# Mixer stage of a two-block kernel: six banks for the first products, values in pairs of blocks, the convolution in two pieces, and an engine order rewritten around them

## The reference, cut to what matters

```python
# second block, one layer; xl 512 latent tokens, xc 256 context tokens
pl = modulate(rmsnorm(xl), sh1, sc1) @ w_in;  pc = modulate(rmsnorm(xc), ...) @ w_in
# mLSTM, 4 heads of 128: q, k from a 3x3 depthwise convolution and silu; v, output gate, input/forget gates
qk = silu(dwconv2d(p[..., :2*W], conv_w, rows, cols))
h_ml = rmsnorm_head(forward scan + backward scan of (q, k, v, gates)) * sigmoid(o)
# HGRN, 4 heads of 128: q = silu(.), decays for two directions, v, gate g
h_hg = rmsnorm_head(forward scan + backward scan of (q, k, v, log decays)) * silu(g)
xl = xl + g1 * (concat(h_ml, h_hg) @ w_out)
# then a convolutional feed-forward part and the final norm
```

## Time and profile before

| | |
|---|---|
| time, median of 3 runs (lowest to highest) | 1871.69 us (1871.32 to 1872.26) |
| the profiled execution: its time, its span | 1873.64 us, 1871.9 us |
| PE busy | 1733.9 us, 93% of the span |
| DVE, ACT, POOL busy | 1176.7, 730.2, 461.1 us |
| mean granted TensorE clock | 0.965 of full speed |
| the stage of the change | about 953 to 1462 us of the span |

### The profile page before, as it was taken

One profiled execution on the slowest core, in us unless ns is written; L12 is line 12 of the kernel. 1 busy time (PEld: TensorE's weight loads), 2 busy tenths in 40 slices (PEclk: granted clock), 3 DMA queues, 4 the chain that ended last, 5 costly groups with the idle time before them and its releaser, 6 DMA issues.

```text
span 1871.9 us, 21559 instructions
## 1 busy us (share of the span) xinstructions
PE 1733.9 (93%) x7645; PEld 1321.3 (71%) x7645; DVE 1176.7 (63%) x2193; ACT 730.2 (39%) x1176; POOL 461.1 (25%) x448
## 2 busy tenths in 40 slices
PE   7998898999989999999998988988898899999996
PEld 3446654588867888888757766877756488888885
DVE  5968653344447755775655377576774587777776
ACT  3154556433443311331253272735361433333224
POOL 2732200030020100110000122221320066656552
PEclk9998799999999999999999999998999999999999
DMA  5264200143333554454303211111311323322311
GB/s 148 68 126 113 76 4 1 45 130 88 108 102 136 184 174 135 161 186 147 123 13 91 57 45 34 53 38 34 102 46 34 101 90 113 113 91 85 118 46 45
DMA packets 185537, 168.69 MB, mean 90 GB/s; under 512 B 17639, under 2 KB 168867, under 8 KB 185051
## 3 DMA queue, kind: packets, MB, share of 16 engines
q1 hardware_dynamic: 173083, 128.19, 22.4%
q0 software_dynamic: 11808, 39.29, 7.1%
q10 hardware_dynamic: 560, 0.12, 0.0%
HBM read 155.83 MB, written 6.31 MB: 87 GB/s over the span
## 4 chain that ended last, share of the span: by engine, by line
PE 71%; DVE 14%; ACT 8%; issue 4%; DMA 1%; POOL 1%; POOLq 0%; DVEq 0%; SPq 0%; ACTq 0%
PE bank L1509 27%; PE bank L1928 18%; PE bank L1620 3%; DVE arena L2678 2%; PE bank L1302 2%; PE bank L1814 2%; DVE arena L3340 2%; PE bank L1669 2%; PE bank L1462 2%; PE bank L1448 2%; PE bank L1625 1%; PE bank L1404 1%; PE bank L1806 1%; DVE arena L3428 1%; PE bank L1660 1%
## 5 line engine op out<-in xcount | busy, mean ns | idle before, releaser
L3582 DVE SCALAR_TENSOR_TENSOR arena<-bank,ffn_taps,arena 128x441 f32<-128x441 f32 (+2 forms) x352 | 220.2, 686 | 79.3 <-ACT arena L2638 79.3
L3049 DVE TENSOR_TENSOR w_lo<-ring,w_hi 128x2048 fp32r<-128x2048 f32 x52 | 119.2, 2292 | 117.0 <-ACT w_hi L2213 113.2
L1509 PE MATMUL bank<-h_lo,w_hi 128*128 128x512 f32 x448 | 176.6, 394 | 3.2 <-DVE w_lo L3049 1.8
L2213 ACT CAST w_hi<-ring 128x2048 fp32r<-128x2048 f32 x52 | 99.2, 1907 | 176.4 <-PE bank L1509 176.4
L1509 PE MATMUL bank<-hT_hi,w_hi 128*128 128x512 f32 x384 | 153.5, 400 | 6.5 <-DVE h_lo L3135 5.8
L1160 POOL TENSOR_TENSOR w_lo<-ring,w_hi 128x2048 fp32r<-128x2048 f32 x21 | 99.7, 4745 | 168.9 <-ACT w_hi L2611 168.9
L1509 PE MATMUL bank<-act_hi,w_hi 128*128 128x512 f32 x352 | 137.9, 392 | 0.2
L1509 PE MATMUL bank<-act_lo,w_hi 128*128 128x512 f32 x352 | 131.8, 389 | 0.0
L1928 PE MATMUL bank<-hT_hi,w_hi 128*128 128x512 f32 x336 | 130.8, 389 | 0.3 <-POOL w_lo L1160 0.3
L1928 PE MATMUL bank<-h_lo,w_hi 128*128 128x512 f32 x336 | 130.7, 389 | 0.0
L1928 PE MATMUL bank<-hT_hi,w_lo 128*128 128x512 f32 x336 | 130.7, 389 | 0.0
(11 more groups left out here) (577 smaller groups left out, 4037.5 us busy)
## 6 DMA issues: line engine op xcount, KB each, us to landing
ring<-in_w_up SPq DMA_DIRECT2D x76, 512.0 KB, 4.6
arena<-in_w_mod POOLq DMA_DIRECT2D x48, 512.0 KB, 4.2
ring<-in_w_in SPq DMA_DIRECT2D x72, 256.0 KB, 3.2
ring<-in_w_down SPq DMA_DIRECT2D x32, 512.0 KB, 4.2
ring<-in_w_in SPq DMA_DIRECT2D x30, 512.0 KB, 3.9
arena<-in_w_down SPq DMA_DIRECT2D x22, 512.0 KB, 4.4
ring<-in_w_out SPq DMA_DIRECT2D x8, 512.0 KB, 3.8
ring<-in_w_out SPq DMA_DIRECT2D x16, 256.0 KB, 3.1
```

The lines of the kernel that those rows point to most:

```text
L1509: ins = pe.matmul(out, u[:, n % SLOTS, cols], v[:, k, :], start=start and k == w[0][0] and m == 0, stop=stop and k == w[-1][0] and m == 2)
L2213: sc.copy(w_hi[:, n % SLOTS, :], ring[:, n % SLOTS, :]).then_inc(hi_ready, 1)
L3049: ve.tensor_tensor(w_lo[:, n % SLOTS, :], ring[:, n % SLOTS, :], value(w_hi[:, n % SLOTS, :]), ALU.subtract)\
L3582: return ve.scalar_tensor_tensor(o[:, ys, xs], x[:, yt, xt], ffn_taps[:, at:at + 1], o[:, ys, xs], ALU.mult, ALU.add)
```

## The change

It has five parts, all in the order of work and the places of tiles; no arithmetic is added or taken away.

1. **Banks.** A new kind "first" goes round six banks (3, 4, 0, 1, 2, 7) and holds all tiles of the prelude up to mlk of head 0, but zc. The decays of head 1 and the rounds use "dense" as before. In the rounds y2 goes to bank 7 (with the HGRN output "o"), y3 to the kind "ml".
2. **Values in pairs.** The four latent blocks of v go in two pairs, each with all high products first; in the last pair low products follow each k. The signals that free chunk slots (`chunk_used` at k = 2, 4, 6) are now given at the first block of the last pair.
3. **Convolution in two pieces.** The query's nine taps (piece 0) run at n = 9, ahead of the first `ml_divide`; the keys' twelve instructions (piece 1) at n = 0 of the round that uses them, after the second `ml_divide`.
4. **Roundings ahead.** In the prelude ACT rounds zf, zb and Vb0 to Vb2 earlier, and DVE takes the lows of zf and zb between the scans of the gate rows, after a memset of `sums` that moves ahead of them. In the rounds ACT rounds g between two halves of `ml_weights`, and mlq ahead of the silus.
5. **Bank reads ahead.** The flips (n = 7) come before the scores s4 and s5 on PE. DVE does `ml_probs` before `assemble` at n = 7 and 8, and `heads_out` ahead of mo's low part at n = 8 (at n = 7 in the last round, ahead of the reads of A6 and A7). ACT copies mlc before mlk.

```diff
--- before.py
+++ after.py
@@ -133 +133,2 @@
-        places = {"unit": (0, 1, 2), "dense": (3, 4), "ml": (5, 6), "o": (7,), "out": (0, 1, 2, 5)}[kind]
+        places = {"unit": (0, 1, 2), "first": (3, 4, 0, 1, 2, 7), "dense": (3, 4), "ml": (5, 6), "o": (7,),
+                  "out": (0, 1, 2, 5)}[kind]
@@ -136,0 +138,5 @@
+    def decays(kind, i):
+        tile(kind, "zf", i)
+        tile("ml", "zc", i)
+        tile(kind, "zb", i)
+
@@ -138 +144 @@
-        tile("dense", "v", 0, b)
+        tile("first", "v", 0, b)
@@ -140 +146 @@
-        tile("dense", "gr", m)
+        tile("first", "gr", m)
@@ -142,8 +148,3 @@
-        tile("dense", "v", 0, b)
-    def decays(i):
-        tile("dense", "zf", i)
-        tile("ml", "zc", i)
-        tile("dense", "zb", i)
-
-    decays(0)
-    tile("dense", "q", 0)
+        tile("first", "v", 0, b)
+    decays("first", 0)
+    tile("first", "q", 0)
@@ -151,2 +152,2 @@
-        tile("dense", "v", 1, b)
-    tile("dense", "cols")
+        tile("first", "v", 1, b)
+    tile("first", "cols")
@@ -154,2 +155,2 @@
-        tile("dense", name, 0)
-    decays(1)
+        tile("first", name, 0)
+    decays("dense", 1)
@@ -178,0 +180,3 @@
+            if n == 7 and i:
+                tile("dense", "fh", i - 1)
+                tile("dense", "fm", i - 1)
@@ -185,3 +188,0 @@
-            if n == 7 and i:
-                tile("dense", "fh", i - 1)
-                tile("dense", "fm", i - 1)
@@ -194 +195 @@
-                    tile("ml", "y", i, b)
+                    tile(("o", "ml")[b - 2], "y", i, b)
@@ -1670 +1671 @@
-                            if (m, b, k, v) == (1, 0, 0, 0) or (last and v == 0 and k in (2, 4, 6)):
+                            if (m, b, k, v) == (1, 0, 0, 0) or (last and n + v == 0 and k in (2, 4, 6)):
@@ -1843,2 +1844,2 @@
-            for b in range(CT, ST):
-                mixer_values(0, [b])
+            for b in range(CT, ST, 2):
+                mixer_values(0, [b, b + 1])
@@ -1851,2 +1852,2 @@
-            for b in range(CT, ST):
-                mixer_values(1, [b])
+            for b in range(CT, ST, 2):
+                mixer_values(1, [b, b + 1])
@@ -1891,0 +1893,3 @@
+                    if n == 7 and i:
+                        hg_flip(i - 1)
+                        ml_flip(i - 1)
@@ -1898,3 +1901,0 @@
-                    if n == 7 and i:
-                        hg_flip(i - 1)
-                        ml_flip(i - 1)
@@ -2488 +2489 @@
-            def ml_weights(i):
+            def ml_weights(i, half):
@@ -2490 +2491 @@
-                for n in range(2 * ST):
+                for n in range(half * ST, (half + 1) * ST):
@@ -2510,2 +2511 @@
-            for b in range(CT + 1, ST - 1):
-                value_copy(0, b)
+            value_copy(0, CT + 1)
@@ -2513 +2512,0 @@
-            value_copy(0, ST - 1)
@@ -2514,0 +2514,2 @@
+            for b in range(CT + 2, ST):
+                value_copy(0, b)
@@ -2515,0 +2517 @@
+            mix_high("Vb0")
@@ -2517,0 +2520,2 @@
+            mix_high("Vb1")
+            mix_high("Vb2")
@@ -2519,2 +2523 @@
-            for k in range(4):
-                mix_high(f"Vb{k}")
+            mix_high("Vb3")
@@ -2528 +2530,0 @@
-            value_copy(1, 4)
@@ -2530 +2531,0 @@
-            value_copy(1, 5)
@@ -2531,0 +2533,2 @@
+            value_copy(1, 4)
+            value_copy(1, 5)
@@ -2540 +2542,0 @@
-            ml_copy("mlk", 0)
@@ -2541,0 +2544 @@
+            ml_copy("mlk", 0)
@@ -2566 +2569 @@
-                        ml_weights(i)
+                        ml_weights(i, 0)
@@ -2567,0 +2571 @@
+                        ml_weights(i, 1)
@@ -2570,0 +2575 @@
+                            mix_high(f"mlq{i + 1}")
@@ -2575,2 +2579,0 @@
-                        if more:
-                            mix_high(f"mlq{i + 1}")
@@ -2592 +2594,0 @@
-                            ml_copy("mlk", i + 1)
@@ -2593,0 +2596 @@
+                            ml_copy("mlk", i + 1)
@@ -3265,0 +3269,2 @@
+            step.mark(ve.memset(sums[:], 0.0))
+
@@ -3286,0 +3292,2 @@
+            mix_low("zf0")
+            mix_low("zb0")
@@ -3291 +3297,0 @@
-            step.mark(ve.memset(sums[:], 0.0))
@@ -3400 +3406 @@
-            def ml_convolve(i):
+            def ml_convolve(i, part):
@@ -3402 +3408 @@
-                for name in ("mlq", "mlk", "mlc"):
+                for name in (("mlq",), ("mlk", "mlc"))[part]:
@@ -3408,2 +3414,3 @@
-                convolve([(qc, ml_q[:, i, :], ROWS, col(0), 1), (kc2[:, C:], ml_k[:, C:], ROWS, col(MH), 1),
-                          (kc2[:, 0:C], ml_k[:, 0:C], 1, col(MH), 1)], qk_conv)
+                convolve([[(qc, ml_q[:, i, :], ROWS, col(0), 1)],
+                          [(kc2[:, C:], ml_k[:, C:], ROWS, col(MH), 1), (kc2[:, 0:C], ml_k[:, 0:C], 1, col(MH), 1)]][part],
+                         qk_conv)
@@ -3487,2 +3494,2 @@
-            for name in ("zf0", "zb0", "q0"):
-                mix_low(name)
+            mix_low("q0")
+            mix_low("Vb0")
@@ -3490 +3497 @@
-            for k in range(4):
+            for k in range(1, 4):
@@ -3494 +3501 @@
-            for name in ("mlq0", "mlk0", "zf1", "zb1"):
+            for name in ("mlq0", "mlk0", "zf1"):
@@ -3496 +3503,2 @@
-            ml_convolve(0)
+            ml_convolve(0, 0)
+            mix_low("zb1")
@@ -3509,0 +3518,2 @@
+                    if n == 8 and i and more:
+                        heads_out(i - 1)
@@ -3512,2 +3522,4 @@
-                    if n == 0 and i:
-                        ml_divide(i - 1, 1)
+                    if n == 0:
+                        if i:
+                            ml_divide(i - 1, 1)
+                        ml_convolve(i, 1)
@@ -3516 +3528 @@
-                    if u <= DIAG:
+                    if u <= DIAG and n not in (7, 8):
@@ -3530,0 +3543,2 @@
+                    if n in (7, 8):
+                        assemble(i, u)
@@ -3534,2 +3548,0 @@
-                    if n == 8 and i:
-                        heads_out(i - 1)
@@ -3538,2 +3551,2 @@
-                    if n == 10 and more:
-                        ml_convolve(i + 1)
+                    if n == 9 and more:
+                        ml_convolve(i + 1, 0)
```

More of the change, by code:

```diff
@@ L2509, in _ @@
             sc.activation(row_b[0:MH], row_b[0:MH], ACT.Ln, bias=1.0).then_inc(ln_ready, 1)
-            for b in range(CT + 1, ST - 1):
+            value_copy(0, CT + 1)
+            mix_high("zf0")
+            mix_high("zb0")
+            for b in range(CT + 2, ST):
                 value_copy(0, b)
-            mix_high("zf0")
-            value_copy(0, ST - 1)
-            mix_high("zb0")
             mix_high("q0")
+            mix_high("Vb0")
             decay_gates(0)
             context_gates(0)
+            mix_high("Vb1")
+            mix_high("Vb2")
             silu(hg_q[:, 0, :], "q", 0)
-            for k in range(4):
-                mix_high(f"Vb{k}")
+            mix_high("Vb3")
             decay_logs(0)
@@ L2527, in _ @@
             exps(1)
+            mix_high("mlq0")
+            mix_high("mlk0")
             value_copy(1, 4)
-            mix_high("mlq0")
             value_copy(1, 5)
-            mix_high("mlk0")
             n = 2 * ST * MH
@@ L2539, in _ @@
             mix_high("zb1")
+            ml_copy("mlc", 0)
             ml_copy("mlk", 0)
-            ml_copy("mlc", 0)
             sc.wait_ge(max_out, 32)
@@ L2591, in _ @@
                         if more:
+                            ml_copy("mlc", i + 1)
                             ml_copy("mlk", i + 1)
-                            ml_copy("mlc", i + 1)
                     if n == 10:
```

## The result

The changed kernel takes 1831.2 us, median of four runs (1829.26 to 1832.88), against 1871.97 us for the kernel before on the same chip: a ratio of 0.9781, 95% interval 0.9768 to 0.9793. On a second chip it was 1828.01 us (1825.48 to 1831.43) against 1873.65, a ratio of 0.9753 (0.9738 to 0.9769). The forecast was 1820 us, with a range of 1807 to 1838. The time is in the range; the gain is 41 to 46 us where 52 were forecast.

What follows compares the result with a forecast made beforehand. The prediction took PE to set the pace, its idle time and clock being what could be won. 38.8 us idle plus 16.0 clock less 3.6 gave 51.2, rounded to 52: 1820 us, range 1807 to 1838.

Steps and rivals of the forecast that it cites:

- zc's 12.8: Rounds: zc's two 6.4 us waits for the bank of y2 or y3 go, gain 12.8 us.
- the 14.1 of scores and mo: At n = 7 and 8: waits of 7.0 and 7.1 us go, less 1.5 new wait, gain 12.6.
- n = 3 of round 0: Unit at n = 3 of round 0: its 6.2 us wait stays, as the diff leaves its cause.
- the loop rival: Rounds held by the POOL, ACT, DVE, PE loop of the units, removed waits return: 1840 us, chance 0.08.
- The sum: Idle time won on PE over prelude and rounds, added by part: 38.8 us.
- y3: Before y3, piece 0 delays the divide: 2.0 us each in three rounds, 6.0 new, bounds 0 and 5.4 each.
- mlq: Rounds: mlq's weights stay behind the context exponentials, leaving about 1.0 us of wait each in rounds 1 and 2.
- The clock: PE's half-clock drops behind waits: 16.0 us won, 3.6 lost at four new waits of about 2 us.
- The second rival: Piece 0 late in full: y3 waits 5.4 us in three rounds, each with a clock drop; 1835 us, chance 0.11.
- The first rival: PE's clock does not come back, many short waits keep the drops, 16 us not won: 1836 us, chance 0.12.
- The prelude: Prelude: eight waits of 10.4 us, gain 9.8 idle, plus 1.75 of clock drop; Vb3's load wait stays.
- The prediction's sign of being wrong: On PE: waits of the same length at other places, units above all, or y3 waits over 6 us.

Runs made afterwards that it cites:

- The pair with the flips: Convolution in two pieces with y2's bank, plus flips, bank reads and heads ahead, on the kernel before: 1845.16 us, ratio 0.9850.
- the convolution alone: Only the convolution in pieces 0 and 1 and y2 in bank 7, on the kernel before: 1853.90 us, ratio 0.9908.
- The casts alone: Only g between the halves of the exponentials and mlq ahead of the silus on ACT, on the kernel before: 1870.70 us, ratio 0.9983.
- piece 0 late: Piece 0 of the convolution moved behind the first divide (n = 10), on the changed kernel: 1820.45 us, ratio 0.9716 to the kernel before.

## Why the prediction was right, and where it was off

**Reading the bound, the old waits and the range: right.** PE set the pace before and after. Each old wait went where the edit said, zc's 12.8, the 14.1 of scores and mo, and the prelude's; n = 3 of round 0 kept 6.2; the outputs of the last round wait 1.90 (forecast 2.2), the unit of round 3 1.31 (1.5), A2 0.4 (0.5). Nothing new stood at another unit, so the loop rival is out.

**The sum: two gains too large, one term missing.** Of idle time 32.4 us went, and 38.8 were forecast: y3 has 4.3 more than in the sum and mlq 3.1, and 1.1 were won beyond it (Vb3's load 0.6, the last outputs 0.3, the unit 0.2). The clock gave 10.9 for 16.0 - 3.6 = 12.4. The remaining 2.7 are no term of the sum. The second rival's 1835 isn't what its terms give: 10.2, and 5.4 less half of it, above 1820 are 1833.

**The clock: right in the net, off in its parts.** Counted by PE's busy time at 0.50, the drops that went were worth 17.9 us (forecast 16.0), and the new ones 6.7 (forecast 3.6). The rule read from the earlier trace rows, a drop behind each wait of 2.2 us and more, doesn't hold for every wait: the gate rows' product of the kernel before waited 2.25 us and had none behind it, and the scores of its last round waited 2.25 us and had one (at 1411.37) that the sum left out. Two errors partly cancel here, which is luck. The first rival, by which 16 us would not be won, is out. The Trainium skill's page "TensorE: Matmul & The Clock Gate", section "A second HAM failure mode: psum-queue depth-cycling", would have kept the drops by the prediction's reading, as more banks are cycled now; the prelude, which cycles six banks, ran at a granted clock of 1.00 (0.99 before), and no round ran at a lower one than before.

**The prelude: 14.1 for 11.6.** Two things were left out. The wait of Vb3's load (0.6) went too. And a wait costs more than its idle time. PE of the kernel before, in order of time:

```profile
964.10 0.39 PE L1841 MATMUL bank<-hT_hi,w_mg_lo 128*128 128x512 f32 x1
965.61 0.50 PE L1669 MATMUL bank<-early_hi,hT_hi 128*128 128x512 f32 x1 [1.13 <-ACT sq L2502]
965.95 0.40 PE L1669 MATMUL bank<-early_hi,m_lo 128*128 128x512 f32 x1
```

A matmul shows 0.39 us but the next starts 0.23 later. From 964.10 to 965.95 are 1.85 us for two steps of 0.23, so the idle of 1.13 cost 1.39. There are nine waits here (the prediction says eight, which are the rows). At 0.26 more each, an estimate from this one, they are 2.3 us, and 11.6 + 0.6 + 2.3 = 14.5, against 14.1.

**y3: the mis-sized term.** "I take 2.0, below the middle, because DVE has 24 to 33 us of idle time in these rounds": three waits came to 10.3 and not 6.0. The average idle share says nothing of the place: DVE's 1.85 us just before y1 were there because PE was late, held by the same waits at n = 7 and 8 that another part of the change takes away. The pair with the flips showed it (10.3 again), and the convolution alone showed the other side (one wait of three, 3.2). The durations did their share: piece 0 6.6 for 6.2, and `decayed` 2.6 for 1.27. The upper bound of 5.4 held, so the second rival, piece 0 late in full, is not reached either. Each of the three had a slow stretch behind it that cost 1.7, where half were counted. The prediction's sign of being wrong, y3 waits over 6 us, is met if it means their sum and not if it means one of them (3.6 at most).

**mlq: the missed step.** "It stays behind the context exponentials ... about 1.0 left in rounds 1 and 2 each": 5.1 us stand there, for another reason. I followed the weights and not the bank. The earlier trace rows name only what came last; with the weights earlier, the bank's read was next, and the same edit pushed it back. The casts alone and q in another bank settle this.

**Why the parts don't add.** 48.8 us of parts are 41 to 46 together. Of the 7.4 lost by convolution and flips, y3's waits are 10.3 - 3.2 = 7.1. q's other bank gave nothing alone and 6.6 us with piece 0 late (1820.45 to 1813.83). Alone, the half clock ate it in the trace, and the one run with a mean clock of 0.974 took 6.8 less than the changed kernel. That the two gains are the same is likely from this, and one run doesn't show it.

**Left open.** Whether a slow stretch stands behind a given wait, and how long it is.

## What to carry to other kernels

Ask of each wait that goes what the engines do at that place once the bound engine is early, and not what they did while it was late: idle time of another engine next to a wait is often made by that wait. When a product's weights come earlier, look next at its bank, who reads it, and whether the edit moved that read. Work of a second engine can be put later only where the bound engine has other work meanwhile. And when an edit does to the waits what was expected and nothing to the time, compare the busy time at half clock before you doubt the edit: here it ate 4.1 us where 3.1 of idle time were won.

## What the runs showed of the hardware

- The two operations of `decayed` took 1.60 and 1.11 us behind piece 0 (the y3 rows above), while POOL ran at the same time (1137.77 to 1141.2), and 0.75 and 0.68 in the convolution alone at 1246.65, where POOL's next instruction came at 1248.36. The sizes are the same. In this stage of nine of the traces the first operation's halves took 0.40 to 0.44 us each, all 509, when POOL did nothing meanwhile, and 0.8 at the median when POOL was busy during most of it (91; some stayed at 0.41). So the longer `decayed` goes with POOL's work; it wasn't tried by itself.
- The same wait of 3.05 us before the same eighteen matmuls was followed by 2.93 us of them in one kernel and 4.24 in another, at one order of work around it. A2's wait of 3.2 us was followed by 6.59 us of eight matmuls in the kernel before and by 3.70, all at full clock, with the casts alone. mlq's 2.18 us had a slow stretch behind it in round 1 of the changed kernel and none in round 2. A forecast of half a drop or one drop for each wait is as fine as these traces allow.
- A tap that needs the one just before it starts 0.72 us after it (128x441, piece 0 in the changed kernel), and 0.59 us in the whole convolution before, where two chains alternate; for 128x504 it is 0.77 and 0.66. Only the context's three taps alternate in piece 1, and the last six are one chain again. The two pieces are 6.6 + 7.0 = 13.6 us for 11.9. By the rule weighed in the prediction, of the Trainium skill's page "VectorE: DVE Perf Modes", section "The DRAIN you can't avoid", that a semaphore after each operation costs nothing extra, they would have been 11.9; for operations that need the one just before them these runs show a cost.
